# Relative-position bias tables: from SyncE's queue in the third nat chunk to ScalarE's queue in the second, five transfers with 8 heads as outer dimension

## The reference

```
h = rmsnorm(x) * (1 + scale) + shift                 # scale, shift, gate from silu(c) @ w_ada + b_ada
p = split(h @ w_in)                                  # q, k, v, gate z of branches A and B, indexer, merge gates
att_a = top-k attention: indexer scores choose min(256, L/4) keys for each query, 8 heads on 2 kv heads
att_b = sliding-window attention over own chunk of 64 and 2 before, with sinks, 8 heads on 2 kv heads
logits = q . k / 8 + rel_bias[t5_bucket(k_pos - q_pos)][head]      # one table of 32 buckets x 16 heads
o_a = (att_a * silu(z_a)) @ w_oa ; o_b = (att_b * silu(z_b)) @ w_ob
y = x + gate * ((sigmoid(g_a) * o_a + sigmoid(g_b) * o_b) @ w_out)
```

## Time and profile before

| | |
|---|---|
| median of 3 runs | 1140.15 us (1138.95 to 1140.45) |
| profiled execution, span from first to last instruction | 1137.2 us |
| TensorE matmul busy | 1038.3 us, 91% |
| VectorE / ScalarE / GpSimd busy | 677.6 / 408.3 / 322.8 us |
| DMA | 120.83 MB, mean 106 GB/s |
| mean granted TensorE clock | 0.950 |

### The profile page before, as it was taken

One profiled execution on the slowest core, in us unless ns is written; L12 is line 12 of the kernel. 1 busy time (PEld: TensorE's weight loads), 2 busy tenths in 40 slices (PEclk: granted clock), 3 DMA queues, 4 the chain that ended last, 5 costly groups with the idle time before them and its releaser, 6 DMA issues.

```text
span 1137.2 us, 18078 instructions
## 1 busy us (share of the span) xinstructions
PE 1038.3 (91%) x6569; PEld 924.0 (81%) x6569; DVE 677.6 (60%) x1437; ACT 408.3 (36%) x1239; POOL 322.8 (28%) x348
## 2 busy tenths in 40 slices
PE   6976999999506999999999999999999999999998
PEld 1346887778306999999999898888888779999998
DVE  2666347899999999999600277645655464332111
ACT  0344556443102232212211467666655452222000
POOL 0043104111002443312213345322311023545442
PEclk9987999999857999999999889999999989999999
DMA  9731002222123322323213562211120536544332
GB/s 356 288 96 43 23 21 95 87 88 76 73 102 126 103 85 82 118 74 102 84 46 133 180 225 85 72 47 52 41 55 20 166 101 196 154 126 126 116 114 73
DMA packets 97490, 120.83 MB, mean 106 GB/s; under 512 B 11104, under 2 KB 79472, under 8 KB 96256
## 3 DMA queue, kind: packets, MB, share of 16 engines
q1 hardware_dynamic: 97408, 119.73, 32.9%
HBM read 89.72 MB, written 35.95 MB: 111 GB/s over the span
## 4 chain that ended last, share of the span: by engine, by line
PE 80%; DMA 8%; issue 4%; DVE 3%; ACT 3%; POOL 2%; POOLq 0%; SPq 0%; DVEq 0%; ACTq 0%
PE PS L1355 17%; PE PS L1357 17%; PE PS L1356 17%; PE PS L1608 9%; DMA snat<-STG 8%; PE PS L1584 6%; PE PS L1529 4%; PE PS L1364 4%; PE PS L1548 2%; PE PS L1587 2%; PE PS L1430 2%; DVE HL L1150 1%; DVE XT L1168 1%; POOL YO L879 1%; PE PS L1534 1%
## 5 line engine op out<-in xcount | busy, mean ns | idle before, releaser
L1355 PE MATMUL PS<-HH,WH 128*128 128x384 f32 (+1 forms) x576 | 189.2, 328 | 52.2 <-POOL WL L774 52.2
L1357 PE MATMUL PS<-HH,WL 128*128 128x384 f32 (+1 forms) x576 | 189.0, 328 | 0.0
L1356 PE MATMUL PS<-HL,WH 128*128 128x384 f32 (+1 forms) x576 | 188.9, 328 | 0.0
L774 POOL TENSOR_TENSOR WL<-RAW,WH 128x512 fp32r<-128x512 f32 (+1 forms) x80 | 100.4, 1260 | 300.2 <-ACT WH L895 300.1
L1209 DVE MAX8 M<-SC 128x8 f32<-128x384 f32 (+3 forms) x210 | 174.8, 870 | 10.5 <-DVE SC L1214 10.0
L1214 DVE MATCH_REPLACE8 SC<-M,SC 128x384 f32<-128x384 f32 (+3 forms) x210 | 179.9, 864 | 0.0
L1355 PEld LDWEIGHTS PS<-HH,WH 128*128 128x128 f32 x576 | 109.1, 189 | 52.7 <-POOL WL L774 52.7
L1355 PE MATMUL PS<-WH,HH 128*128 128x512 f32 (+3 forms) x288 | 110.3, 383 | 8.1 <-DVE HL L1150 7.9
L1356 PEld LDWEIGHTS PS<-HL,WH 128*128 128x128 f32 x576 | 109.0, 189 | 0.0
L1357 PEld LDWEIGHTS PS<-HH,WL 128*128 128x128 f32 x576 | 109.0, 189 | 0.0
L1356 PE MATMUL PS<-WL,HH 128*128 128x512 f32 (+3 forms) x288 | 108.7, 377 | 0.0
(11 more groups left out here) (180 smaller groups left out, 2068.1 us busy)
## 6 DMA issues: line engine op xcount, KB each, us to landing
RAW<-in_w_all SPq DMA_DIRECT2D x72, 256.0 KB, 2.7
WADA<-in_w_ada SPq DMA_DIRECT2D x8, 1536.0 KB, 20.1
gz<-STG SPq DMA_DIRECT2D x48, 192.0 KB, 1.8
snat<-STG SPq DMA_DIRECT2D x24, 256.0 KB, 2.0
QKV<-snat SPq DMA_DIRECT2D x8, 768.0 KB, 5.9
GT<-gz SPq DMA_DIRECT2D x32, 192.0 KB, 2.5
XN<-in_x_prompt SPq DMA_DIRECT2D x8, 512.0 KB, 16.8
btad<-bvd SPq DMA_DIRECT2D x4, 1024.0 KB
```

The costliest lines, as they stand in the source:

```text
L774: nc.gpsimd.tensor_tensor(WL[c % 2][:, k, 0:cw], RAW[:, n % 4, 0:cw], WH[c % 2][:, k, 0:cw].bitcast(F32), ALU.subtract).then_inc(lo_done, 1)
L1355: T.matmul(out, wh, mh, start=first, stop=False)
L1356: T.matmul(out, wh, ml, start=False, stop=False)
L1357: return T.matmul(out, wl, mh, start=False, stop=last)
```

## The change

The four transfers of 2 heads by 1024 columns become four of 8 heads by 256 columns; the fifth keeps its shape. All five are issued by ScalarE in chunk 2, one behind each of the first five weight conversions of chunk 3's tiles, after a wait for bvd. SyncE's code for them goes. The semaphore that was counted for bvd and gated together is split, and SyncE waits for gated before it loads GATE.

```diff
-        scratch_out = sem("scratch_out")
+        bvd_out = sem("bvd_out")
+        gated_out = sem("gated_out")
...
-            sp.dma_start(bvd, BV[:, :]).then_inc(scratch_out, 16)
+            sp.dma_start(bvd, BV[:, :]).then_inc(bvd_out, 16)
...
-            sp.dma_start(gated, GROW[:]).then_inc(scratch_out, 16)
+            sp.dma_start(gated, GROW[:]).then_inc(gated_out, 16)
...
-                if c == 3:
-
-                    if j == 0:
-                        sp.wait_ge(scratch_out, 32)
-                    if j < 4:
-                        sp.dma_start(btad[:, 2 * j:2 * j + 2, :].rearrange("p h j -> h p j"),
-                                     bass.AP(bvd.tensor, 2 * BIAS_L * j + 127, [[BIAS_L, 2], [-1, 128], [1, 1024]])).then_inc(bias_out, 16)
-                    elif j == 4:
-                        sp.dma_start(btbd.rearrange("p h j -> h p j"), bass.AP(bvd.tensor, 8 * BIAS_L + 895, [[BIAS_L, 8], [-1, 128], [1, 256]])).then_inc(bias_out, 16)
...
                 if i == 6:
+                    sp.wait_ge(gated_out, 16)
...
+            def bias_table(j):
+
+                if j < 4:
+                    cols, dst, first = slice(256 * j, 256 * j + 256), btad, 127 + 256 * j
+                else:
+                    cols, dst, first = slice(0, 256), btbd, 8 * BIAS_L + 895
+                act.wait_ge(bvd_out, 16)
+                nc.scalar.dma_start(dst[:, :, cols].rearrange("p h j -> h p j"),
+                                    bass.AP(bvd.tensor, first, [[BIAS_L, 8], [-1, 128], [1, 256]])).then_inc(bias_out, 16)
+
             for p, (c, j, w) in enumerate(PIECES):
...
                 if j < KD:
                     w_hi(KD * (c + 1) + j)
+                if c == 2 and j < 5:
+                    bias_table(j)
```

## The result

The changed kernel takes 1084.28 us (median of 4 runs, 1083.33 to 1085.92) against 1139.67 us for the kernel before in the same comparison: ratio 0.9516, 95% interval 0.9503 to 0.953. 1085 was predicted, faster. The profiled execution spans 1081.5 us, 55.7 less than the one of before; 55.0 was the sum.

The account below looks back on a forecast made before the run. The hole before chunk 4 was taken as bound by two DMA engines carrying tables, with chunk 3's stores and chunk 4's weights queued behind. 1140.15 - 52.2 (wait) - 2.8 (clock) + 0 = 1085 us, range 1082 to 1102.

Parts of the forecast that it names:

- rival 5: Attention: the cover behind the masks is gone or its first loads are late; some 10 us back, 1095 us; chance 0.03.
- Rivals 3 and 4: Tables: 1 KB pieces cost as much as 4 KB (chance 0.02), or eight heads do not spread (0.01); either 1153 us.
- G: Time for one table in chunk 2 beside stores and loads: 8.2 us, bounds 6.4 and 18.0.
- the lower bound of 4.9: Least time in us for a table alone on eight engines, at 26.5 GB/s per engine; 6.3 was taken.
- ScalarE's lateness: Chunk 2: ScalarE held at its table issues, 8.4 us late at the fifth, covered by PSUM, at no cost.
- what would show it: Signs of being right: no TensorE wait over 1.5 us starting chunks 3 and 4, ScalarE's later table issues about 8 us apart.
- Rival 1: Chunk 2: ScalarE is held at its own table issues, so chunk 3 starts late; put at 1094 us, chance 0.22.
- Rival 4's price: Tables stay on two engines, 21.1 us per MB: 1153 us, also for the move to ScalarE without the spread; chance 0.01.
- Rival 2: Chunk 2: SyncE's transfers wait behind ScalarE's tables though in another queue; put at 1091 us, chance 0.17.
- The clock in the rivals: Late chunk 3 start: the clock costs its 2.8 us again only if TensorE idles over 3.6 us.

Follow-up runs that it names:

- e8: The changed kernel without the five table expansions and the wait for them, the bias read from x_prompt instead: 1085.82 us, 0.9521 of the kernel before.
- e1: The changed kernel with its 8-head tables issued by SyncE in chunk 3, where the kernel before issued its own: 1084.32 us, 0.9508 of the kernel before.
- e6: The changed kernel with all five tables issued behind the first piece of chunk 2: 1087.91 us, 0.9547 of the kernel before.
- e4: The changed kernel with tables of 4 heads by 512 columns on four engines, the fifth unchanged: 1094.24 us, 0.9623 of the kernel before.

## Why the prediction was right

**The size of the gain.** 52.2 us of wait and 2.8 of clock were to go, nothing to come in their place: 55.0 against 55.7 in span and 55.4 in the medians. That the tables would cost nothing is shown by e8, that nothing later takes it back by the window from 299.2 to 580 and by the mask's 19.4 us, so rival 5 falls too.

**Eight engines.** Read off the share of 0.52 in the earlier trace rows; the packet counts and e1 confirm it. Rivals 3 and 4 fall.

**The price of a table** was too high: G = 8.2 us was taken, and five tables ran from about 208.4, a microsecond after the first issue, to 247.1, 7.7 each. The table alone was 6.3 us from the mixed window of the earlier trace rows, and 5.35 in e6; the lower bound of 4.9 was nearer than the value that I chose. The share left beside stores and loads was off the other way: 0.77 was taken, and 5.35 of 7.7 is 0.69. The two errors partly cancelled. By the prediction's sum the forecast holds for any G below 8.8, so they did not decide it.

**ScalarE's lateness** was wrong, on the safe side. I had it 8.4 us late at the fifth table, issued by 239.2; it was let go at 232.57 and was late for nothing. Beside G, two terms did it. The queue holds 0.84 of a table, not the 0.53 that I had worked out from the earlier trace rows; with it 208.4 + 3.16 x 7.7 = 232.7, which is what happened, without the 1.2 us that I had added for the issue itself. And the issue does not stand behind the conversion in front of it but runs beside it, so the first table started at 208.4 and not at 209.5. So the line in "what would show it", issues about 8 us apart, was wrong: they are 5.44 us apart, and none of them delays a piece.

**Rival 1** is real but needs more: four engines (e4) or all five at once (e6).

**Rival 4's price** was tried by e2, the move to ScalarE without the spread. It took 1129.93 us, not 1153: the price went by G = 27.4, and the tables of e2 took 21.0, as they did on SyncE's queue. The move does not make a table faster.

**Rival 2** falls. The Trainium skill, "Perfetto Trace Analysis", section "DMA Instruction — HWDGE (DVE, Sync)", has the generator shared and locked for one instruction at a time; if so, SyncE's weight loads in e2 should have waited for the end of ScalarE's 20 us. They took 0.33 us. The measurement decides: a ScalarE issue that waits for room in its queue keeps nothing from SyncE.

**The clock in the rivals** was priced wrongly. From one stop in the earlier trace rows I took it that the clock costs something only if TensorE idles for over 3.6 us. In e6 a stop of 1.8 us was followed by a fall: the clock went down at about 232.1 (0.93 on the mean from 230.90 to 232.25), when TensorE had been running again for 1.2 us, and was 0.50, 1.2 GHz, from there to past 235.2.

## What to carry to other kernels

A transfer that runs on few engines shows in the windows as a small, constant share (0.13 is two of sixteen) while its queue is stuck; look at the issue time of the transfer behind it, not at its own. Before moving such a transfer to another queue, change its outermost dimension, or set the transfers further apart: each alone gave the full 55 us here, and the other queue alone gave 10. What a held queue costs is the excess over the buffers on the path from it to the busy engine. Follow the chain to find which buffers those are: here the three STG buffers, some 14 us, and not the four PSUM banks.

## What was not expected of the hardware

- A held issue moves, it does not go away: with tables of 21 us on ScalarE's queue its instructions stop for 20.06 us at a time (e2), as SyncE's store did before.
- The clock can fall after a stop that is already over (e6: stop from 229.1 to 230.9, clock 0.50 from about 232.1).
- By the reading above, a queue took 0.84 of a table of 1 KB pieces ahead (108 of an engine's 128), against 0.53 worked out for pieces of 4 KB. Why the two differ was not tried.
